# Weaving the second block's two token mixers between the slots of its input projection, with columns in another order

## What is computed

```
gq, gk, gv, gz, gg, rq, rk, rv, rg = split(h @ w_in)          # 256 x 3616
log_a = log_sigmoid(gz @ gate_w + gate_b) / 16                # forward and backward
o_gf, _ = gla_chunked(gq, gk, gv, log_a[:, :, 0], s_gf)       # 4 heads, chunks of 64 tokens
o_gb, _ = gla_chunked(flip(gq), flip(gk), flip(gv), flip(log_a[:, :, 1]), s_gb)
o_rf, _ = retention_chunked(rope(rq), rope(rk), rv, log_gamma[0], s_rf)
o_rb, _ = retention_chunked(flip(rq), flip(rk), flip(rv), log_gamma[1], s_rb)
o_g = head_rmsnorm(o_gf + flip(o_gb)) * silu(gg)
o_r = head_layernorm(o_rf + flip(o_rb)) * silu(rg)
out = concat(o_g, o_r) @ w_out
```

## Time and profile before

| | |
|---|---|
| Time, median of 3 runs | 1522.93 us (1517.28 to 1523.43) |
| The profiled execution's own time | 1516.76 us |
| Its span in the trace | 1514.9 us |
| PE busy / DVE busy / ACT busy | 1052.4 / 547.6 / 288.2 us |
| w_in's slots | 597.9 to about 680 us |
| The mixers | about 680 to 805 us |
| w_out's slots | 805.3 to 830.4 us |
| First expert matmul | 868.9 us |

### The profile page before, as it was taken

One profiled execution on the slowest core, in us unless ns is written; L12 is line 12 of the kernel. 1 busy time (PEld: TensorE's weight loads), 2 busy tenths in 40 slices (PEclk: granted clock), 3 DMA queues, 4 the chain that ended last, 5 costly groups with the idle time before them and its releaser, 6 DMA issues.

```text
span 1514.9 us, 12849 instructions
## 1 busy us (share of the span) xinstructions
PE 1052.4 (69%) x5326; PEld 602.9 (40%) x5326; DVE 547.6 (36%) x1030; ACT 288.2 (19%) x459; POOL 47.8 (3%) x60
## 2 busy tenths in 40 slices
PE   0888958699889896993867665655556565556574
PEld 0666747476656685872635411111111111111121
DVE  6965765575423695437665400000000000000002
ACT  3322433452412333424022200000000000000000
POOL 0010000000000001004110000000000000000000
PEclk8897987799999998995657697677887778787887
DMA  9894202476434485530003499999999999999994
GB/s 387 321 366 173 99 29 84 176 285 272 140 111 167 146 344 213 188 141 12 1 0 125 167 413 425 428 426 427 426 426 428 427 426 425 428 427 426 425 428 203
DMA packets 40858, 415.01 MB, mean 274 GB/s; under 512 B 4896, under 2 KB 4896, under 8 KB 7648
## 3 DMA queue, kind: packets, MB, share of 16 engines
q1 hardware_dynamic: 38160, 405.75, 66.0%
q10 hardware_dynamic: 2640, 8.44, 1.5%
HBM read 413.13 MB, written 1.05 MB: 273 GB/s over the span
## 4 chain that ended last, share of the span: by engine, by line
PE 42%; DMA 38%; DVE 12%; ACT 4%; issue 2%; POOL 1%; DVEq 0%; POOLq 0%; ACTq 0%
DMA ring<-in_w_egu 24%; DMA ring<-in_w_ed 12%; PE PS L593 7%; PE PS L595 7%; PE PS L594 7%; PE PS L1177 4%; PE PS L870 3%; PE PS L529 3%; DVE ringR L1340 2%; DVE arena L1223 2%; ACT ringR L2147 1%; DMA ring<-in_w_in 1%; PE PS L1208 1%; PE PS L704 1%; DVE ring L1265 1%
## 5 line engine op out<-in xcount | busy, mean ns | idle before, releaser
L1177 PE MATMUL PS<-ring,arena 128*32 128x512 f32 (+1 forms) x1536 | 234.3, 747 | 154.8 <-DMA ring<-in_w_egu 153.8
L593 PE MATMUL PS<-ringR,arenaR 128*128 128x512 f32 (+1 forms) x520 | 216.8, 417 | 44.1 <-DVE arenaR L1328 43.2
L595 PE MATMUL PS<-ringR,arenaR 128*128 128x512 f32 (+1 forms) x520 | 211.1, 406 | 0.0
L594 PE MATMUL PS<-ringR,arenaR 128*128 128x512 f32 (+1 forms) x520 | 210.7, 405 | 0.0
L1340 DVE TENSOR_TENSOR ringR<-ring,ringR 128x2048 fp32r<-128x2048 f32 (+1 forms) x66 | 148.6, 2254 | 119.3 <-ACT ringR L2147 119.3
L1223 DVE SCALAR_TENSOR_TENSOR arena<-arena,PS 128x256 f32<-128x256 f32 (+2 forms) x68 | 33.3, 497 | 415.3 <-ACT arena L2536 399.5
L1177 PEld LDWEIGHTS PS<-ring,arena 128*32 128x32 f32 x1536 | 49.7, 130 | 332.2 <-DMA ring<-in_w_egu 250.5
L1208 PE MATMUL PS<-ring,arena 128*32 128x512 f32 x704 | 118.5, 809 | 81.0 <-DMA ring<-in_w_ed 80.3
L529 PE MATMUL PS<-CT,arena 128*128 128x128 f32 (+1 forms) x352 | 68.0, 350 | 131.9 <-ACT arena L2125 39.0
L2147 ACT ACTIVATE ringR<-ring 128x2048 fp32r<-128x2048 f32 (+1 forms) x66 | 123.4, 1882 | 146.3 <-PE PS L595 108.0
L593 PEld LDWEIGHTS PS<-ringR,arenaR 128*128 128x128 f32 x520 | 101.9, 196 | 73.1 <-DVE arenaR L1328 44.7
(11 more groups left out here) (315 smaller groups left out, 891.0 us busy)
## 6 DMA issues: line engine op xcount, KB each, us to landing
ring<-in_w_egu SPq DMA_DIRECT2D x64, 2048.0 KB, 26.3
ring<-in_w_ed SPq DMA_DIRECT2D x44, 2048.0 KB, 25.7
ring<-in_w_egu SPq DMA_DIRECT2D x32, 1536.0 KB, 20.9
ring<-in_w_vad SPq DMA_DIRECT2D x40, 1024.0 KB, 7.0
ring<-in_w_in SPq DMA_DIRECT2D x22, 1024.0 KB, 5.4
ring<-in_w_gu SPq DMA_DIRECT2D x22, 1024.0 KB, 4.8
ring<-in_w_dn SPq DMA_DIRECT2D x10, 1024.0 KB, 4.8
ring<-in_w_ada SPq DMA_DIRECT2D x8, 1024.0 KB, 8.6
```

Source lines behind the costliest of these rows:

```text
L593: mm(o, xh(k, t), hi[:, c], start=k == 0, stop=False)
L594: mm(o, xh(k, t), s.viewr[:, c], start=False, stop=False)
L595: i = mm(o, xl(k, t), hi[:, c], start=False, stop=k == nk - 1)
L1177: i = mm(PS[32 * ee:32 * ee + 32, b + a_, 0:fw], XEv[:, k, 32 * E:32 * E + 32], wv[:, ee, a_, :], start=k == 0, stop=k == 7, tile_position ...
```

## The change

- The groups of w_in come in the order gq gk, rq, rk, gv, rv, gg, rg. Both token tiles have one PSUM bank each (2 and 7), so the four banks that the mixers use are free from the start.
- w_in is a third lane `w` (14 steps), woven with `g` (18 steps), `r`, `d` (the decay masks, now DVE's) and `t` (the gates, now DVE's) by the string `GLA`. On PE the first step is `pre`, ahead of w_in's first slot.
- w_in and w_out stream through 4 raw slots instead of 8; slots 4 to 8 are the mixers' scratch. The experts' first pair goes into slots 4 and 5 once retention's outputs are transposed. Early loads (`gw2`, `gateb2`, a new `posr`, `gnorm`) are issued by ACT before w_in.
- GLA's states of four heads and both directions lie in one compact tile; one pair of operations updates them all, with combined factors `Ff`. Before, each of 2 directions x 2 head pairs took 4 operations on 128x256 with a mask of blocks in each of 4 steps.
- Retention: the scores' product and the two state terms are summed in PSUM (the queries are scaled beforehand in `TH`), and ACT copies the sum. Before, DVE read three results per head and tile.
- Squares are whole rows on ACT with a reduction on DVE instead of 16 short activations with accumulators. w_out's slots are sorted by k, so the first two need only GLA's half; retention's output transposes stand behind the first of them, and `gate_rows(3)` moves from w_in's seventh slot to behind w_out's third.

```diff
-G_IN2 = [(0, 512), (512, 512), (1056, 512), (1568, 512), (2080, 512), (2592, 512), (3104, 512)]
+G_IN2 = [(0, 512), (1568, 512), (2080, 512), (512, 512), (2592, 512), (1056, 512), (3104, 512)]
...
+PLAN["out2"].sort(key=lambda x: x[1])
...
-    n = {"g": 17, "r": 17}
-    gla = weave(dict.fromkeys(n, 0), n, {}, "gr", "gr")
...
+GLA = "g w d g w g d w g w g g w g w r g w g w r g w g r w g r w g r w g r t w g r g r g w g r t r".split()
...
-            s = n % NROT if n < first_moe else 2 * ((n - first_moe + (first_moe % NROT + 1) // 2) % ((NRAW + NHIGH) // 2))
+            if n == first_moe:
+                for x in range(KEPT, NRAW):
+                    holder[x] = ("mixer", None)
+            if n < first_moe:
+                s = min(range(NROT if n < first_in2 else KEPT), key=lambda x: -1 if holder[x] is None else turn[holder[x]])
+            else:
+                s = (4, 6, 0, 2, 8, 10)[(n - first_moe) % 6]
...
# PE
+            def w_in2():
+                def free(g, t):
+                    if g:
+                        return [at("v in2 ev" if t else "a in2 ev", g - 1)]
+                    return [at("a gate row", 1), at("v dn y", 1)]
+                for n, _ in enumerate(dense("in2", tile(rnd(HH4)), tile(rnd(hT2)), lambda g, t: 7 if t else 2, free)):
+                    if n == 0:
+                        gate_rows(2, 4)
+                    yield
...
                 for s in range(4):
+                    if s < 3:
+                        w.wait_ge(*(at("v gla tk", s - 1) if s else at("v gla pm", 1, 1)))
+                        for d in range(2):
...
+                            for r in range(2):
+                                for hh in range(2):
+                                    i = mm(PS[64 * hh:64 * hh + 64, d, 128 * r:128 * r + 128], KN[z:z + 64, d, c // 2, 128 * r + 64 * hh:128 * r + 64 * hh + 64],
+                                           pjv[z:z + 64, c // 2, 512 + 256 * r + 128 * hh:640 + 256 * r + 128 * hh], start=True, stop=True)
+                        i.then_inc(*sig("pe gla st", s))
...
+                        for t in range(2):
+                            o = PS[:, 6, 128 * t:128 * t + 128]
+                            for j in range(2):
+                                mm(o, p[:, 256 * j + 128 * t:256 * j + 128 * t + 128], pjv[:, j, 2464 + 128 * h:2592 + 128 * h], start=j == 0, stop=False)
+                            for d in range(2):
+                                q = TH[:, 1024 * d + 256 * (h - 1) + 128 * t:1024 * d + 256 * (h - 1) + 128 * t + 128]
+                                i = mm(o, q, SR[:, 256 * (h - 1) + 128 * d:256 * (h - 1) + 128 * d + 128], start=False, stop=d == 1)
+                        i.then_inc(*sig("pe ret o", h - 1))
...
+            for n, _ in enumerate(dense("out2", lambda k, t: hh2[k // 4](k % 4, t), tile(rnd(hT2)), lambda g, t: 4 * t + g,
+                                        lambda g, t: [at("v gla ot"), at("a gla ot")])):
+                if n == 0:
+                    next(lanes["r"])
+                if n == 2:
+                    w.wait_ge(*at("a in2 ev", 6))
+                    gate_rows(3, 2)
...
# DVE
+            def decays():
+                w.wait_ge(*at("a ret dm"))
+                tt(DM, DM, TH, ALU.mult).then_inc(*sig("v ret"))
...
+                def states(s, x):
+                    for z in range(2):
+                        q = slice(64 * z, 64 * z + 64)
+                        i = tt(KEq[q, :, SXD[s % 2][z], :], x[q], Ff[q, 4 * s:4 * s + 4].unsqueeze(2).broadcast_to([64, 4, 128]), ALU.mult)
+                    i.then_inc(*sig("v gla sx", s))
...
-                            ts(Sx, Sg, emid, None, ALU.mult).then_inc(*sig("v gla sx", s, d, r))
...
-                                tt(tk, PS[:, m % 2, 0:256], C("BM"), ALU.mult).then_inc(*sig("v gla tk", m))
-                                chain()
-                                tt(tk, tk, Sx, ALU.add).then_inc(*sig("v gla"))
-                                chain()
-                                ts(Sg, tk, eend, None, ALU.mult).then_inc(*sig("v gla"))
...
-                        cp(o, PS[:, b, 0:128]).then_inc(*sig("v ret"))
-                        chain()
-                        stt(o, PS[:, b, 128:256], GAv[:, t, 0, h:h + 1], o, ALU.mult, ALU.add).then_inc(*sig("v ret"))
-                        chain()
-                        stt(o, PS[:, b, 256:384], GAv[:, t, 1, h:h + 1], o, ALU.mult, ALU.add).then_inc(*sig("v ret o", h, t))
...
# POOL
-                e.tensor_tensor(dm, dm, t_, ALU.mult).then_inc(*sig("g ret"))
-                e.tensor_tensor(dm[:, 0:128], dm[:, 0:128], ident, ALU.add)
-                e.tensor_tensor(dm[:, 384:512], dm[:, 384:512], ident, ALU.add).then_inc(*sig("g ret dm", h))
...
-                    e.tensor_scalar(th_, th_, 0.5, 0.5, ALU.mult, ALU.add).then_inc(*sig("g ret"))
-                    e.tensor_tensor(gg, gg, th_, ALU.mult).then_inc(*sig("g ret"))
-                    i = e.tensor_tensor(gg, gg, gn[:, 512 * n:512 * n + 512], ALU.mult)
```

599 lines of the change are left out of this document (303 added, 296 removed).

## The result

The changed kernel takes 1458.28 us (median of 4 runs, 1454.83 to 1458.77); the kernel before, in the same rounds, 1522.91 (1517.28 to 1523.43). The ratio is 0.958, with a 95% interval from 0.955 to 0.961. The sign and the place were right; the size was not.

The account below looks back on a forecast made before the run. Experts bound by transfers; ahead of them the mixers are a chain across engines, none full. Terms sum to 175 us against 232.5, 57.5 less; 12.5 for clock leaves a gain of 45: 1477 us, range 1460 to 1500.

Parts of the forecast that it names:

- (a): Start of w_in on PE: `pre` now comes first and waits for DVE's copy of z, 4.2 us, no cover.
- term (f): PE's clock over the whole path: 8.3 us for four cold starts and 4.2 in the weave, 12.5 us lost.
- (b): From `pre` to L: slot, gate rows, ACT's decays and DVE's masks take 22.5 us, PE idling some 7.5 ahead of `kn`.
- (c): Woven middle, `kn` to retention's last scores: PE is the bound, 94.8 us of work plus waits, 99.5 us.
- The rope's price: Rope on DVE in the woven middle: 24 operations take 8.6 us, the low price, with products off POOL.
- (d): From the last scores to retention's normed output: DVE is the bound, 27.6 us of work and 1.5 of waits, 29 us.
- (e): The end, to w_out's end: retention's transposes, three slots and gate rows, 19.8 us.
- The window from 830.4: From w_out's end to the experts: nothing to gain; savings ahead of 868.9 should move the end by as much.
- A: Rival: short fp32 matmuls between slots keep PE's clock at 0.5, some 1588 us, slower; chance 0.05.
- B: Rival: PE waits for copies at each of six w_in group changes, 24 us lost, about 1502; chance 0.17.
- C: Rival: clock stays at 1.00, ACT's and DVE's waits shorter, gain 57 or more, 1465 or below; chance 0.12.
- D: Rival: the expert stage is late for another reason, a first pair not there, so no change; chance 0.02.

Follow-up runs that it names:

- experiment 2: Changed kernel with `st` in its old shape, four matmuls of 128 output partitions and 256 columns a step instead of eight smaller: 1458.94 us.
- experiment 4: Changed kernel with every `st` matmul issued four times, neighbours in one quarter of the array in the first step, alternating in the others: 1463.6 us, one run.
- experiment 11: Changed kernel with the two dropped tables of constants (256 and 4 columns) put back, unused: 1464.47 us.
- experiment 12: Changed kernel with 260 unused columns behind the constants in SBUF alone, so the weights' ring starts at byte 20604: 1468.16 us, ratio 0.967.
- experiment 13: Changed kernel with the table of constants 260 columns wider in DRAM alone, SBUF unchanged: 1457.82 us, ratio 0.961.
- experiment 5: Changed kernel with retention's decays moved behind the steps that make L and `kn`: 1455.67 us.
- experiment 6: Changed kernel with the decays later as in experiment 5, w_in's first slot ahead of `pre`, and `kn` moved: 1442.8 us, ratio 0.948.
- experiment 1: Changed kernel with w_in's fourteen slots in one piece, not woven with the mixer steps, the reworked operations kept: 1490.7 us, ratio 0.982.
- experiment 9: Both kernels measured and profiled once more, unaltered: the kernel before 1517.36 us, the changed kernel 1457.31 us.
- experiment 15: Kernel before with 97 unused columns of constants in SBUF, so its ring starts at byte 20992: 1514.01 us, ratio 0.998.

## Why the prediction was wrong in size

I take its steps from PE's first w_in matmul, which stood 4.6 us behind the first z matmul before, and so at 600.8 after. To w_out's end the prediction had 175 + 12.5 = 187.5 us; it is 175.8. Of the expert stage it said nothing would change.

- **(a) first step, 4.2:** 4.3 (605.12 - 600.8). Right, and `pre` took 3.75 at half clock, as term (f) had it. (Its price per cold start comes from one execution: twelve slow matmuls at w_out's start; the kernel before, run again, has six there.)
- **(b) to L, 22.5, with 3.3 of clock:** 26.0 (605.12 to 631.14), with the wait of 7.4 where 7.5 was forecast. Right.
- **(c) the woven middle, 99.5 and 8.2 of clock, together 107.7:** 96.2. **This is the step that failed**, by 11.5 us, in two of its terms. The price of the short matmuls: `st` was taken at 8 x 0.24 = 1.9 a step and `in` at 4 x 0.455 = 1.8, both from matmuls that use the whole array, and they take 0.61 and 1.02. Over three and four steps that is 3.9 + 3.2 = 7.1 us too much. Experiments 2 and 4 show why: such matmuls run beside one another. And the clock: 4.2 were set aside for a weave at a clock between 0.91 and 1.00. The windows of 10 us show what was granted:

```profile
660.00:670.00 10.00, 10.00 (x52) 8.38 (x52) 9.71 (x20) 2.52 (x2) 0.00 (x0) 1.00 0.46 166
670.00:680.00 10.00, 6.27 (x29) 5.39 (x28) 9.53 (x18) 1.91 (x1) 0.00 (x0) 0.83 0.29 106
680.00:690.00 10.00, 9.49 (x67) 8.43 (x66) 8.03 (x7) 3.59 (x4) 0.00 (x0) 1.00 0.32 107
690.00:700.00 10.00, 10.00 (x61) 7.52 (x60) 5.00 (x7) 1.91 (x1) 0.00 (x0) 1.00 0.31 106
```

  From 640 to 740 every window but the one with the rope's wait has 1.00. The rows show no clock lost to the weave itself; what was lost stands behind the waits at `kn` and at the scores. 7.1 and 4.2 are 11.3 of the 11.5. PE's idle time in this part was 4.5 us (96.2 less 91.7), as forecast, with 3.7 at the scores where 2.5 was forecast and less elsewhere. The rope's price held: 24 operations in 9.0 us, 0.42 each, with nothing of POOL's beside them.
- **(d) DVE's tail, 29:** 28.1. Right. **(e) the end, 19.8 and 1 of clock:** 21.3. Right.
- **The window from 830.4, "nothing to gain there":** the expert stage became 3.8 us shorter in the first pair of profiles, by the rate of its transfers. Experiments 11 to 13 show that the place of the buffers in SBUF does it; that this start had moved was in the change (fewer constants), and I had looked only at what instructions do. By medians it is 7 to 10 us (1464.5 against 1457.3, and 1468.2 against 1457.8). With the old places the kernel takes 1464.5, 57.1 less than the kernel before of its rounds: inside the range, and nearly the 57.5 that the sum had with no clock lost.
- **The base:** off the profiled execution, 1516.8 - 45 = 1472 was forecast and 1458.8 came, 13 us less: 11.7 of the path, 3.8 and 0.3 from w_out's end on, less 2.9 up to z. The medians differ by 64.6 in the first rounds, and by 64.3 between the changed kernel run again and the kernel before of its rounds (1521.6). But the kernel before had medians from 1514.9 to 1522.9 in five sets of rounds, so of the 18.7 us by which the prediction missed, some 6 are of the size of that spread.

The rivals. A (half clock) was the opposite of what happened. The rule of the Trainium skill that it cited ("TensorE: Matmul & The Clock Gate", "What's actually happening"), that activity releases the throttle, agrees with the trace: from 640 to 740 only the window with a wait of 3.7 us was below 1.00, at 0.83. B (a wait at each change of group) didn't show in the changed kernel: PE waits there for no copy of a w_in group. In the orders of experiments 5 and 6 it did, with 1.0 to 2.4 us at one or two changes. C (no cold starts, shorter tail) gave the right size by luck: the cold starts came and the tail was as forecast, but the matmuls and the weave were cheaper. D fell. No wait for ring slots showed, and POOL's products are gone (24.7 us busy, before 47.8 by its page).

The gain is the weave's by half to three fifths and the reworked operations' by the rest, which experiment 1 alone shows. And the changed kernel left some 16 us on the table: its waits (a) and (b) come from where the first two slots and the decays stand in a list of letters, and an order without them takes 1440.9 to 1442.8 us.

## What to carry to other kernels

Price a matmul by its rows and output partitions too, not by its columns alone, and look for a record of that very shape, or take the range down to a third. Where dense slots can be laid between the short steps of a chain, ask which wait is left ahead of each: here those waits, not the weave, cost the clock, and moving a few letters of the order was worth 14 us, half as much as all the reworked operations. When a wait is moved by reordering, read where it turns up: twice here (rope) it came back in full at a later step. And a change that drops a constant moves every buffer behind it, which was alone worth half a per cent here.

## What the hardware showed that I had not expected

- Matmuls of 64 rows by 64 output partitions, 128 columns of fp32: 0.076 us each in a step of eight over all four quarters, 0.102 in a step of 32 with neighbours alternating between two, 0.187 with eight in a row in one quarter; 64 by 128 with 256 columns 0.27, 128 by 64 with 256 columns 0.255, against 0.455 for the whole array, all at a granted clock of 1.00. `in` (128 by 64) follows `st` (64 by 64) with no gap in the rows (695.56 behind 694.95, a step's own 0.61).
- The rate of the weights' transfers at 97% busy DMA engines goes with the buffers' place in SBUF: 430 to 431 GB/s with the ring at byte 19564 of each partition (twelve profiles, one of them with other places in DRAM), 427 to 428 at 19968, 20604 and 20992 (six profiles). From w_out's last product to the end the twelve take 677.5 to 681.0 us and the six 682.9 to 687.1. The bytes are counted from the declared sizes.
- From 640 to 740, where PE changes between slots and matmuls of 4 to 256 columns, its granted clock was 1.00 in nine windows of 10 us, with no wait of PE's over 0.51 us, and 0.83 in the one with a wait of 3.7 us. That waits alone set it isn't shown: in the kernel before no wait from 741 to 781 us was over 1.3 us, and yet the clock was 0.50 from 760 to 780, and 0.67 and 0.83 at the same place in the profiles of experiments 9 and 15.
